# Row terms and mask of an mLSTM head as two 512-column products, ahead of key by query

## The reference, cut to what matters

```
b = jnp.cumsum(lfc, -1)
dmat = jnp.where(causal, b[..., :, None] - b[..., None, :] + lic[..., None, :], -jnp.inf)
m_inter = b + m[..., None]
m_t = jnp.maximum(m_inter, dmat.max(-1))
s = jnp.einsum('bhtd,bhsd->bhts', qc, kc) * jnp.exp(dmat - m_t[..., None])
num = w_inter[..., None] * jnp.einsum('bhtd,bhde->bhte', qc, C) + jnp.einsum('bhts,bhse->bhte', s, vc)
```

## Time and profile before

| | |
|---|---|
| median of 3 runs | 1083.84 us |
| lowest and highest | 1078.72 and 1086.41 us |
| profiled execution, its own time | 1077.93 us |
| its span, first to last instruction | 1076.2 us |
| mean granted TensorE clock | 0.879 |
| PE busy | 911.1 us (85%) |
| DVE busy | 424.9 us (39%) |
| ACT busy | 206.0 us (19%) |

### The profile page before, as it was taken

The page is one execution under the profiler, slowest core; times in us unless marked ns, Lnnn a source line. Parts: engine busy times, 40 slices in busy tenths (PEclk is TensorE's granted clock), DMA queues, the critical chain, the costliest instruction groups (busy, mean ns, idle before and its releaser), DMA issues.

```text
span 1076.2 us, 16056 instructions
## 1 busy us (share of the span) xinstructions
PE 911.1 (85%) x6653; PEld 603.8 (56%) x6653; DVE 424.9 (39%) x843; ACT 206.0 (19%) x470; POOL 168.9 (16%) x268
## 2 busy tenths in 40 slices
PE   1999999999989776888888899739999999999800
PEld 1678888887767654777886354514444444444300
DVE  6433345526546864554534443550000000000067
ACT  3311231322212221111112011101111112111111
POOL 8100000001247205220040100010000000000043
PEclk9989999999999667688767799659999999999955
DMA  9142222222101111100004700687999999999261
GB/s 254 35 141 59 60 59 59 59 60 67 33 14 28 42 43 30 40 1 1 2 1 163 207 24 36 237 304 269 386 400 375 404 403 398 412 393 423 94 204 68
DMA packets 74564, 169.16 MB, mean 157 GB/s; under 512 B 16684, under 2 KB 50064, under 8 KB 70160
## 3 DMA queue, kind: packets, MB, share of 16 engines
q1 hardware_dynamic: 61668, 145.64, 37.2%
q0 software_dynamic: 4496, 15.86, 4.9%
q10 hardware_dynamic: 8348, 6.93, 2.1%
HBM read 150.92 MB, written 17.50 MB: 156 GB/s over the span
## 4 chain that ended last, share of the span: by engine, by line
PE 77%; DVE 11%; ACT 2%; issue 2%; DMA 1%; POOL 1%; ACTq 0%; POOLq 0%; DVEq 0%
PE banks L1691 15%; PE banks L2113 11%; PE banks L1686 7%; PE banks L2109 6%; PE banks L2133 6%; PE banks L2038 5%; PE banks L2128 3%; DVE arena L1360 2%; PE banks L1883 1%; PE banks L2094 1%; PE banks L1882 1%; PE banks L1695 1%; PE banks L1873 1%; PE banks L2054 1%; PE banks L1764 1%
## 5 line engine op out<-in xcount | busy, mean ns | idle before, releaser
L1691 PE MATMUL banks<-arena 128*128 128x288 f32 x704 | 178.6, 415 | 0.7 <-ACT arena L738 0.7
L1691 PEld LDWEIGHTS banks<-arena 128*128 128x128 f32 x704 | 135.9, 195 | 38.0 <-ACT arena L738 0.8
L2113 PE MATMUL banks<-arena 128*64 128x512 f32 x544 | 120.5, 596 | 0.0
L1570 DVE TENSOR_TENSOR arena<-arena,banks 128x128 f32<-128x128 f32 (+1 forms) x34 | 12.1, 356 | 269.3 <-ACT arena L985 269.3
L2113 PEld LDWEIGHTS banks<-arena 128*64 128x64 f32 x544 | 37.6, 137 | 74.9 <-issue 74.9
L1686 PE MATMUL banks<-arena 128*128 128x128 f32 (+1 forms) x640 | 74.0, 276 | 0.0
L1686 PEld LDWEIGHTS banks<-arena 128*128 128x128 f32 (+1 forms) x640 | 71.9, 181 | 1.6
L646 POOL DMA_INDIRECT arena<-x_rows,arena x17 | 15.7, 925 | 346.0 <-PE banks L2094 235.3
L2109 PE MATMUL banks<-arena 128*32 128x256 f32 x1088 | 63.5, 386 | 0.9 <-ACT arena L971 0.9
L2133 PE MATMUL banks<-arena 128*64 128x512 f32 x272 | 62.1, 599 | 0.0
L2038 PE MATMUL banks<-arena 128*128 128x512 f32 x128 | 57.8, 612 | 5.0 <-ACT arena L936 5.0
(11 more groups left out here) (493 smaller groups left out, 1418.4 us busy)
## 6 DMA issues: line engine op xcount, KB each, us to landing
arena<-we_gate SPq DMA_DIRECT2D x17, 2048.0 KB, 15.4
arena<-we_up SPq DMA_DIRECT2D x17, 2048.0 KB, 20.1
arena<-we_down SPq DMA_DIRECT2D x17, 2048.0 KB, 20.8
arena<-w_in SPq DMA_DIRECT2D x30, 512.0 KB, 4.0
y_slots<-arena ACTq DMA_DIRECT2D x34, 128.0 KB, 8.1
arena<-w_out SPq DMA_DIRECT2D x1, 4096.0 KB, 12.8
y_slots<-arena ACTq DMA_DIRECT2D x68, 32.0 KB, 10.3
arena<-x_prompt SPq DMA_DIRECT2D x4, 512.0 KB, 8.1
```

Source lines behind the costliest of these rows:

```text
L1570: dve.tensor_tensor(hid[:, part], hsl[:, part], up, ALU.mult).then_inc(q_["hid_ready"], 1)
L1691: ins = pe.matmul(out[:, c], w[:, k, :], xT[:, k, c], start=k == 0, stop=k == KD - 1)
L2113: ins = pe.matmul(A[64 * q:64 * q + 64, :].rearrange("p (g f) -> p g f", g=2), xsT[p_][:, k, 0:64], wgu[:, :, k, 256 * q:256 * q + 256], s ...
```

## The change

The four row-term products of the prompt tiles become one product of 512 columns, and so do the four mask products: `neg_p` is read four times over through a broadcast pattern. The two products of the sample tile stay. All four now stand ahead of the five key by query products, follow the wait for `k_tokens` alone and signal a new semaphore, `log_weights`. ACT waits for that in place of `scores`. DVE, which reads the scores in bank 4, now waits for `scores` itself.

```
                 if h < HA - 2:
                     to_raw(26 + 2 * h)
-                act.wait_ge(q_["scores"], h + 1)
+                act.wait_ge(q_["log_weights"], h + 1)
                 for i in range(TILES):
...
                 dve.tensor_copy(C0[:, :, 128], ncol.rearrange("p (b h) -> p b h", h=HA)[:, :, h]).then_inc(q_["v_spread"], 1)
+                dve.wait_ge(q_["scores"], h + 1)
                 dve.wait_ge(q_["weights"], h + 1)
...
                 if h < HA - 2:
                     slot(26 + 2 * h)
+                pe.wait_ge(q_["k_tokens"], h + 1)
+                pe.matmul(bank[6][:, :], sel[0:HA, h, :], rbm[0:HA, 0:SEQ], start=True, stop=False)
+                pe.matmul(bank[6].rearrange("p (i t) -> p i t", i=PT), ident, neg_p.unsqueeze(1).to_broadcast([128, PT, 128]), start=False, stop=True)
+                pe.matmul(bank[7][0:NS, 128:192], sel[0:HA, h, 0:NS], rbm[0:HA, SEQ:N], start=True, stop=False)
+                pe.matmul(bank[7][0:NS, 128:192], ident[0:NS, 0:NS], neg_s[0:NS], start=False, stop=True).then_inc(q_["log_weights"], 1)
                 pe.wait_ge(q_["q_scaled"], h + 1)
-                pe.wait_ge(q_["k_tokens"], h + 1)
                 for i in range(TILES):
-                    n = rows(i)
                     kq = bank[4][:, 128 * i:128 * i + 128] if i < PT else bank[5][0:NS, NS:2 * NS]
-                    dd = bank[6][:, 128 * i:128 * i + 128] if i < PT else bank[7][0:NS, 128:192]
-                    pe.matmul(kq, kT[h % 2][:, cols(i)], qT[h % 2][:, cols(i)], start=True, stop=True)
-                    pe.matmul(dd, sel[0:HA, h, 0:n], rbm[0:HA, cols(i)], start=True, stop=False)
-                    ins = pe.matmul(dd, ident[0:n, 0:n], neg_p if i < PT else neg_s[0:NS], start=False, stop=True)
+                    ins = pe.matmul(kq, kT[h % 2][:, cols(i)], qT[h % 2][:, cols(i)], start=True, stop=True)
                 ins.then_inc(q_["scores"], 1)
```

## The result

The changed kernel took 1065.4 us in the median of 11 runs (1062.3 to 1072.6), the one before 1079.3 us in the 11 runs beside it (1073.6 to 1093.1). The ratio is 0.9882, 95% interval 0.985 to 0.9914. On a second occasion the same changed kernel took 1069.9 us (12 runs) against 1077.4, ratio 0.9941, interval 0.9901 to 0.9982. Over all runs of this study the median before is 1079.8 us (120 runs, 1070.1 to 1093.6) and with the change 1068.4 us (23 runs, 1062.3 to 1080.8): 11.4 us less.

The account below looks back on a forecast made before the run. PE was taken as three quarters of what sets the end, with waits for ACT in heads 2 and 3. The terms 1.5 + 1.5 - 1.5 + 1.6 + 3.9 + 1.2 = 8.2 us, off 1083.84, gave 1075.6 us, range 1069 to 1082.

Parts of the forecast that it names:

- the sum: Over the four heads and the clock: 1.5 + 1.5 - 1.5 + 1.6 + 3.9 + 1.2 = 8.2 us less.
- Rival B: DVE slips past POOL's selects and the clock rises in head 3's block: 11.5 us less, 1072.3 us; chance 0.27.
- The step that failed: Stages behind the heads only move along; 8.2 us off the runs' median of 1083.84 gives 1075.6 us.
- The clock in the heads: PE's block at the full clock in heads 0 and 1, at 0.50 in head 2.
- The prices: PE's block at full clock 3.5 us against 5.08; at half clock 6.55 against 9.04; mask product 1.0 at full clock.
- Head 1 and POOL: Head 1 gains 1.5 us on PE, but POOL's selects hold DVE behind it, so 1.5 us are given back.
- rival D: The clock fails to rise in head 1, whose slots take 16 us, not 8: 8 to 16 us more; chance 0.05.
- Head 2: PE could be 3.9 us earlier, but DVE is late next: the numerator starts 1.6 us earlier, PE waiting some 2.
- Head 3: No convolution, DVE done early, so PE sets the pace and all 3.9 us are gained.
- The rise of the clock: In head 3 the level rises sooner, before or in the numerator: 0 to 2.4 us, taken as 1.2.

Follow-up runs that it names:

- the best version: The change plus products nobody reads at PE's waits, vpad of head 2 behind the state's carrying, POOL's selects behind head 1's stores: 1061.0 us, ratio 0.9843.
- its dense form: The best version with the unread products multiplying the projection's input by itself in place of the identity by the mask: 1059.9 us, ratio 0.983.
- change with fillers: The change plus products into unused bank 0 that nobody reads, where PE waits in heads 1, 2 and 3: 1067.7 us, ratio 0.9903.

## Why the prediction was wrong, point by point

**The number.** The forecast's 1075.6 and the measured 1065.4 are 10.2 us apart. 4.5 of them are the base: the three runs of before had a median of 1083.8, the 11 beside the change 1079.3, and all 120 have 1079.8. The other 5.7 are the gain, 8.2 forecast and 13.9 measured. That excess was not in the heads. In the two first profiles the four heads gained 1.0, -0.8, 1.7 and 4.9 us, 6.8 together, where the sum had 1.5, 0, 1.6 and 5.1; in the second profile of the change they gained 4.6 us. Rival B, 1072.3, lay nearest, but not by its mechanism: DVE did not slip past POOL's selects, and in head 3 the level rose only behind the block.

**The step that failed** is the sum's last one. It took the median of three runs as the base, and put all stages outside the heads at nothing: "Nothing behind the heads depends on an absolute time: the next stages start from the end of head 3 (`cs_new`) and move along." The runs show in its place that these stages, with the same code, take 281.9 to 289.6 us ahead of the heads and 191.7 to 203.7 behind them, by the clock that is granted. Between the two first profiles they differ by 6.8 us in all, half of it ahead of the heads, where the change can't reach. Their averages are the same with narrow and with wide products, so as far as 14 profiles tell, this is chance that the first occasion had in its favour. On the second the gain was 6.4 us by the ratio (2 to 10.7), below the 8.2. The range, down to 1069, was drawn about a base 4.5 us too high and had nothing for this spread.

**The clock in the heads** was taken from one profile as well, with the blocks of heads 0 and 1 always at the full clock. The runs show that a narrow block can lose the level, in 4 of 10 over all kernels with narrow products, 1 of 6 in the kernel before itself, and that the wide one at its own length never did, in 18. One such fall costs 1.6 us in its block and slot. Over two heads that is 0.5 us on average at 1 of 6, and 1.3 at 4 of 10. So the change may gain a little more than the sum had; whether it does at all, the two occasions, 12.7 and 6.4 us, don't settle, and it stays open.

**The prices.** Block at the full clock: 3.5 us forecast, 3.97 measured, as key by query takes 1.35 us for five, not 1.05, and the row term 1.06, not 0.96. So heads 0 and 1 gain 1.1 us each, not 1.5. The mask product: 1.0 forecast, 1.05 measured. At half the clock: 6.55 forecast, 7.22 measured (362.54 - 355.32), of which 0.3 is in the two wide products (2.0 each, not 1.85) and 0.36 in key by query. The row behind the 1.85, L1695 with 1.78 us, had begun before the level was down; the same product wholly at half the clock takes 1.87 (319.44 to 321.31 in the third profile of before).

**Head 1 and POOL.** The hold was there, but at another place: POOL's chain had come earlier, the selects ran from 345.64 to 349.20, and held DVE's convolution instead (both of one timeline):

```profile
344.61 3.47 DVE L1179 SCALAR_TENSOR_TENSOR arena<-arena 128x600 f32<-128x600 f32 x3
...
350.18 0.17 DVE L1278 COPY arena<-arena 128x8 f32<-128x8 f32 x1
```

L1278 was not held; the convolution L1179 was, for 0.9 us (2.60 in head 0), of which 0.41 reached PE. In the second profile of the change it took 4.34 us, and 1.43 reached PE. The head gave its gain back, 35.0 us against 34.2, as the sum had it, but that is luck in part. The block gained 1.1, and 1.5 were lost through a longer stretch at half the clock at the head's start, which no term had (rival D's mechanism, at 1.5 us in place of 8 to 16): its first product took 2.07 us where it was 1.14, and the slot behind the transposes 9.40 us in place of 8.84. From the head's start to its block it was 11.23 us in two profiles of before and 13.60 in the third, and 12.5 to 12.9 in the six of the change, of merging alone and with vpad or the selects moved: those two profiles had a short stretch, and the prediction rested on one of them. POOL's place was known too roughly, and it had started 1.5 us earlier against the head because its stores landed sooner (a wait of 3.41 us in place of 4.90).

**Head 2.** 1.6 us forecast, 12.33 - 10.81 = 1.5 measured. PE waits 1.50 us for DVE, forecast some 2, and the run with vpad moved shows that DVE's queue was the reason.

**Head 3.** 3.9 us forecast up to the numerator, 12.33 - 8.64 = 3.7 measured, no wait for DVE. 0.5 of that is already the clock, which rose as `c_delta` began (1.42 us in place of 1.88); in the second profile, where it did not, it is 12.33 - 9.09 = 3.2. So 3.2 us are the block and the wait for ACT, less than forecast by what the prices above lacked. The rise of the clock: 1.2 forecast; the numerator up to `cs_delta` took 4.89 us in place of 6.10, so 1.2 measured, and 1.7 with the 0.5.

**The parts.** By the ratios nearly all of the gain is the merging's: 0.9914 alone, against 0.9994 for the order alone, where 5.6 and 2.8 us had been expected. The profiles say why. Up to the numerator of heads 2 and 3 the order alone saves 1.5 and 1.7 us, the merging alone 1.6 and 1.8 (10.72 and 10.56 in place of 12.33), and both together 1.5 in head 2, where DVE is late, and 3.7 in head 3. But the order's narrow products let the clock fall in heads 0 and 1, at 6.6 us more. Order alone was profiled once.

## What to carry to other kernels

Merge small products that share their weights, and count the gaps: at the full clock four pairs of 128 columns took 3.3 us, two products of 512 took 2.1. Ask what is late next on each engine before you price a wait: in the second profile of the change, at half the clock, head 3 reached its numerator in 9.09 us and head 2 in 10.81, so DVE's queue took 1.7 of 3.2 us. And where one profile shows a clock level, take a second and a third before you build on it; two of before agreed to 1 us, the third lay 12 us off. A forecast of 8 us on 1080 needs its base from many runs, and a range about it for the stages that it leaves alone.

## What the runs showed of the hardware

- PE without a gap does not always keep its clock, nor raise it. Under row terms on 4 rows and masks through an identity it fell from 1.00 to 0.51 with PE busy for all of the 17 us that followed; in the next head the same products ran 12.4 us at 1.00; in the two after that they stayed at 0.50 for 23 us. Under dense products of the same 512 columns it stayed at 1.00 twice and rose from 0.50 twice.
- A moving operand read four times over through a step of zero costs the same as a plain one: the fillers, two products in a row of either kind, took 1.98 us at the full clock both times. First the mask through a step of zero, in the best version, then the data, in its dense form:

```profile
318.06 1.98 PE L1748 MATMUL banks<-arena 128*128 128x512 f32 x4
313.24 1.98 PE L1748 MATMUL banks<-arena 128*128 128x512 f32 x4
```

- POOL's two selects, run beside DVE, stretched a `tensor_scalar` from 0.47 to 1.55 us and a `tensor_tensor` from 0.69 to 1.61 (change with fillers), and three `scalar_tensor_tensor` from 2.60 to 4.34 (second profile of the change).
- Products of 128 columns took 0.27 us each with five of a kind in a row, and 0.41 when weights of 4 and of 128 rows took turns.
- Code that is the same took 282 to 290 us ahead of the heads and 192 to 204 behind them, by the clock that was granted.
